# A decoder step on one core: sample keys by sorted lists, low halves of the projection on VectorE

## What is computed

```python
def _select_keys(scores, qpos, kpos, topk):
    admissible = kpos[None, None, :] <= qpos[None, :, None]
    scores = jnp.where(admissible, scores, -jnp.inf)
    _, idx = lax.top_k(scores, topk)
    valid = idx <= qpos[None, :, None]
    return idx, valid
...
    p, new_pool = _pool_mixer(u, pool_buf, pos0, pool_w, pool_scale)
    mix = jnp.concatenate([a, p.astype(a.dtype)], axis=-1)
    x = x + _rmsnorm(jnp.einsum('btm,md->btd', mix, w_o), g_mix_post)
    f, new_conv = _conv_ffn(_rmsnorm(x, g_ffn_pre), conv_buf, w_up, conv_w, conv_b, w_down)
    x = x + _rmsnorm(f, g_ffn_post)
```

## Time and profile before

| What | us |
|---|---|
| median of three runs (lowest, highest) | 1237.61 (1235.37, 1239.82) |
| the profiled execution, its span | 1237.51, 1235.7 |
| TensorE busy | 1165.7 (94%) |
| VectorE busy | 853.7 (69%) |
| ScalarE busy | 540.1 (44%) |
| GpSimd busy, of it low halves | 162.5 (13%), 97.3 |

### The profile page before, as it was taken

One profiled execution on the slowest core, in us unless ns is written; L12 is line 12 of the kernel. 1 busy time (PEld: TensorE's weight loads), 2 busy tenths in 40 slices (PEclk: granted clock), 3 DMA queues, 4 the chain that ended last, 5 costly groups with the idle time before them and its releaser, 6 DMA issues.

```text
span 1235.7 us, 25937 instructions
## 1 busy us (share of the span) xinstructions
PE 1165.7 (94%) x9153; PEld 1121.5 (91%) x9153; DVE 853.7 (69%) x1495; ACT 540.1 (44%) x769; POOL 162.5 (13%) x109
## 2 busy tenths in 40 slices
PE   8999977988989799999999999999999899999993
PEld 7889967966879699999999999999999899999992
DVE  4779899877447877777777777777776444444445
ACT  7333322434224664555545545455454343434341
POOL 4746765200000400000000000000000000000002
PEclk9999988999899999999999999999999899999997
DMA  8987856735885175555555555555556666666641
GB/s 300 319 262 252 274 182 205 252 121 174 293 290 178 36 241 194 168 181 181 166 188 169 179 182 168 187 170 176 185 166 194 203 182 180 179 185 175 185 138 70
DMA packets 81080, 238.76 MB, mean 193 GB/s; under 512 B 9440, under 2 KB 28992, under 8 KB 78704
## 3 DMA queue, kind: packets, MB, share of 16 engines
q1 hardware_dynamic: 75152, 225.40, 57.2%
q10 hardware_dynamic: 4480, 9.01, 2.2%
q0 software_dynamic: 1408, 3.84, 0.9%
HBM read 231.64 MB, written 24.16 MB: 207 GB/s over the span
## 4 chain that ended last, share of the span: by engine, by line
PE 83%; DVE 11%; DMA 3%; ACT 1%; issue 1%; SPq 0%; DVEq 0%; POOL 0%; ACTq 0%; POOLq 0%
PE bank L1312 26%; PE bank L1313 26%; PE bank L1315 26%; DVE lo L406 1%; DMA cache_ring<-vscr 1%; DVE Ws L976 1%; DVE part L1184 1%; DVE top8s L975 1%; DMA raw<-in_w_in 1%; DMA x<-xscr 1%; DVE mixed L1016 1%; PE bank L1488 1%; PE bank L1523 1%; DVE short L1084 1%; DVE mixed L1022 1%
## 5 line engine op out<-in xcount | busy, mean ns | idle before, releaser
L1312 PE MATMUL bank<-h_hi,hi 128*128 128x266 f32 (+1 forms) x2096 | 606.9, 290 | 18.1 <-DVE kT L1040 7.4
L1315 PE MATMUL bank<-h_hi,lo 128*128 128x266 f32 (+1 forms) x2096 | 604.8, 289 | 0.0
L1313 PE MATMUL bank<-h_lo,hi 128*128 128x266 f32 (+1 forms) x2096 | 604.1, 288 | 0.0
L406 DVE TENSOR_TENSOR lo<-raw,hi 128x1024 fp32r<-128x1024 f32 (+2 forms) x322 | 384.1, 1196 | 210.6 <-ACT hi L398 187.2
L398 ACT ACTIVATE hi<-raw 128x1024 fp32r<-128x1024 f32 (+2 forms) x362 | 373.4, 1034 | 320.8 <-PE bank L1315 267.4
L1312 PEld LDWEIGHTS bank<-h_hi,hi 128*128 128x128 f32 x2096 | 399.5, 191 | 23.6 <-issue 19.3
L1313 PEld LDWEIGHTS bank<-h_lo,hi 128*128 128x128 f32 x2096 | 398.1, 190 | 0.1
L1315 PEld LDWEIGHTS bank<-h_hi,lo 128*128 128x128 f32 x2096 | 397.6, 190 | 0.0
L1312 PE MATMUL bank<-g_hi,hi 128*128 128x264 f32 x704 | 200.3, 285 | 5.7 <-DVE lo L406 5.7
L1313 PE MATMUL bank<-g_lo,hi 128*128 128x264 f32 x704 | 201.2, 286 | 0.0
L1315 PE MATMUL bank<-g_hi,lo 128*128 128x264 f32 x704 | 200.3, 284 | 0.0
(11 more groups left out here) (239 smaller groups left out, 788.9 us busy)
## 6 DMA issues: line engine op xcount, KB each, us to landing
raw<-in_w_up SPq DMA_DIRECT2D x176, 512.0 KB, 3.8
raw<-in_w_in SPq DMA_DIRECT2D x56, 512.0 KB, 5.3
raw<-in_w_down SPq DMA_DIRECT2D x64, 448.0 KB, 3.4
raw<-in_w_o SPq DMA_DIRECT2D x32, 512.0 KB, 4.3
raw<-in_w_down SPq DMA_DIRECT2D x32, 512.0 KB, 3.6
kscr<-in_cache_k SPq DMA_DIRECT2D x64, 128.0 KB
vscr<-in_cache_v SPq DMA_DIRECT2D x64, 128.0 KB
mixed<-kscr SPq DMA_DIRECT2D x8, 512.0 KB, 6.5
```

What stands on the lines that cost most here:

```text
L406: ops.tensor_tensor(lo[:, s, 0:width], raw[:, s, 0:width], hi[:, s, 0:width].bitcast(F32), ALU.subtract).then_inc(done, 1)
L1312: mm(out, w_hi, x_hi[:, k, first:], start=(opens and done == 0), stop=False)
L1313: mm(out, w_hi, x_lo[:, k, first:], start=False, stop=False)
L1315: last = mm(out, w_lo, x_hi[:, k, first:], start=False, stop=(closes and done == total))
```

## The change

- **Low halves.** All chunks' low halves are made by VectorE; GpSimd's loop is gone. In front of its work for tile t VectorE makes the two low halves of tile t + 1 (`low_halves`). ScalarE's first high halves of the projection stand a little earlier.
- **Sample keys.** TensorE sums the sample scores into 64 rows of 128 scores: eight lists per sequence. `sample_lists` gives half the lists the opposite sign and puts the scores back in one row per sequence. Sixteen `sort_round`s order all lists at once. `merge_lists` and `merge_quarters` keep maxima and minima of pairs of lists and put them in order by comparisons at halving distance (`compare`); `sample_threshold` finds the 256th score, and three mask steps make the mask, ties by a running sum.
- **Order.** One unit per tile: a prompt round at U0, U1 and U3 to U7 and at the first two query tiles, `sample_lists` at U2, a pooling group at K0 to V1, now in front of the copy, the prompt mask at the third query tile, four sort rounds at each of the next four, `merge_lists` at the last. The first six heads have the rest.

The diff, cut to its core:

```diff
-        if cj < C_PROJ:
-            eng.wait_ge(lo_dve, 4 * r + cj + 1)
-        elif cj < C_WOP:
-            eng.wait_ge(lo_pool, 4 * r + cj - C_PROJ + 1)
-        else:
-            eng.wait_ge(lo_dve, 4 * r + cj - (C_WOP - C_PROJ) + 1)
+        eng.wait_ge(lo_dve, 4 * r + cj + 1)
...
-            with pool.Fori(0, (C_WOP - C_PROJ) // 4) as i:
-                for j in range(4):
-                    lo_chunk(pool, nc.gpsimd, lo_pool, i, C_PROJ + j)
...
+            hi_chunk(ae, 0, C_PROJ)
+            hi_chunk(ae, 0, C_PROJ + 1)
             for h in range(12, 16):
                 relu_head(h, h % 2)
-                hi_chunk(ae, 0, C_PROJ + h - 12)
+                if h < 14:
+                    hi_chunk(ae, 0, C_PROJ + h - 10)
...
-                if t in range(2, 7):
+                if t in range(2, 8):
                     lo_chunk(dve, nc.vector, lo_dve, 0, C_IQ + 2 * t + 2)
                     lo_chunk(dve, nc.vector, lo_dve, 0, C_IQ + 2 * t + 3)
...
+                if h == 13:
+                    lo_chunk(dve, nc.vector, lo_dve, 0, C_PROJ + 2)
+                    lo_chunk(dve, nc.vector, lo_dve, 0, C_PROJ + 3)
...
-            def sample_round(n):
-                src = (Ss if n == 0 else Ws)[:, :]
-                st.link(nc.vector.max(top8s[:, :], src))
-                st.link(nc.vector.match_replace(Ws[:, :], top8s[:, :], src, NEG))
+            def sample_lists():
+                dve.wait_ge(ssum_done, 1)
+                st.then(nc.vector.tensor_copy(Ss[:, PAST:CTX], misc[0:DB, 0:1]))
+                st.link(nc.vector.tensor_scalar(scored, bank[2][:, 0:LIST], con[:, SGN:SGN + 1], None, mul))
+                st.link(nc.vector.stream_shuffle(other, scored, NEXT_ROWS))
+                for c in range(8):
+                    q = slice(32 * (c // 2), 32 * (c // 2) + DB)
+                    src = (other if c % 2 else scored)[q]
+                    st.then(nc.vector.tensor_scalar(Ss[:, LIST * c:LIST * (c + 1)], src, list_sign(c), None, mul))
+                st.wait()
+            def sort_round(n):
+                src = scored if n == 0 else rest
+                st.link(nc.vector.max(ranked[:, 8 * n:8 * n + 8], src))
+                if n < LIST // 8 - 1:
+                    st.link(nc.vector.match_replace(rest, ranked[:, 8 * n:8 * n + 8], src, NEG))
+            def compare(dst, src, d, rows):
+                to, of = (x[0:rows].rearrange("p (n t d) -> p n t d", t=2, d=d) for x in (dst, src))
+                st.then(nc.vector.tensor_tensor(to[:, :, 0, :], of[:, :, 0, :], of[:, :, 1, :], ALU.max))
+                st.link(nc.vector.tensor_tensor(to[:, :, 1, :], of[:, :, 0, :], of[:, :, 1, :], ALU.min))
+            def merge_lists():
+                st.link(nc.vector.tensor_copy(partner[0:64, 0:LIST], ranked[64:128]))
+                for half, pick in ((0, ALU.max), (1, ALU.min)):
+                    st.then(nc.vector.scalar_tensor_tensor(merged[0][0:64, LIST * half:LIST * (half + 1)],
+                                                           partner[0:64, 0:LIST], -1.0, ranked[0:64], mul, pick))
+                st.wait()
+                for n in range(7):
+                    compare(merged[1 - n % 2], merged[n % 2], 64 >> n, 64)
+            def merge_quarters():
+                st.link(nc.vector.tensor_copy(partner[0:32], merged[1][32:64]))
+                st.link(nc.vector.scalar_tensor_tensor(merged[0][0:32], partner[0:32], -1.0, merged[1][0:32],
+                                                       mul, ALU.max))
+                st.link(nc.vector.tensor_scalar(merged[0][0:32], merged[0][0:32], con[0:32, FLIP:FLIP + 1], None, mul))
+            def compare_quarters(n0, n1):
+                for n in range(n0, n1):
+                    compare(merged[1 - n % 2], merged[n % 2], 128 >> n, 32)
+            def sample_threshold():
+                st.link(nc.vector.stream_shuffle(partner[0:32], merged[0][0:32], NEXT_ROWS))
+                st.link(nc.vector.scalar_tensor_tensor(lowest, merged[0][0:DB], -1.0, partner[0:DB], mul, ALU.min))
+                st.link(nc.vector.max(top8s[:, :], lowest))
+                st.link(nc.vector.scalar_tensor_tensor(thr[:, 1:2], Ss[:, PAST:CTX], -1.0, top8s[:, 1:2], mul, ALU.max))
+                st.link(nc.vector.tensor_tensor(thr[:, 1:2], thr[:, 1:2], top8s[:, 0:1], ALU.min))
+                st.link(nc.vector.tensor_scalar(thr[:, 0:1], thr[:, 1:2], -1.0, None, mul))
+            def sample_mask_1():
+                st.link(nc.vector.tensor_scalar(Ws[:, :], Ss[:, :], thr[:, 0:1], None, ALU.is_gt))
+                st.then(nc.vector.reduce_sum(thr[:, 2:3], Ws[:, :], AX.X))
+                st.link(nc.vector.tensor_scalar(among, Ss[:, :], thr[:, 0:1], None, ALU.is_equal))
+            def sample_mask_2():
+                st.link(nc.vector.tensor_tensor_scan(among, among, among, thr[:, 2:3], ALU.add, ALU.max))
+                st.link(nc.vector.tensor_scalar(among, among, float(TOPK_S), None, ALU.is_le))
+            def sample_mask_3():
+                st.link(nc.vector.scalar_tensor_tensor(among, Ss[:, :], thr[:, 0:1], among, ALU.is_equal, mul))
+                st.link(nc.vector.tensor_tensor(Ws[:, :], Ws[:, :], among, ALU.add))
+                nc.vector.tensor_scalar(Ws[:, :], Ws[:, :], -1.0, -MASKED, ALU.add, ALU.mult).then_inc(smask_ready, 1)
...
+            def low_halves(t):
+                for j in range(2):
+                    lo_chunk(dve, nc.vector, lo_dve, 0, C_PROJ + 2 * t + j)
...
             for t in range(U0, U0 + 8):
-                for _ in range(3 if t < 2 else 1 if t < 5 else 0):
+                if t:
+                    low_halves(t + 1)
+                if t == 2:
+                    sample_lists()
+                else:
                     prompt_round(next(rounds_p))
                 ps = tile_ready(t)
...
             for t in range(K0, K0 + 4):
+                low_halves(t + 1)
+                pool_group(t - K0)
                 ps = tile_ready(t)
                 dst = kT[:, t - K0, :] if t < V0 else vT[:, t - V0, :]
-                ins = nc.vector.tensor_tensor(dst, ps[:, 0:T], rms[:, :], mul)
-                ins.then_inc(tile_freed, 1)
-                pool_group(t - K0)
-                if t < V0:
-                    sample_round(next(rounds_s))
+                nc.vector.tensor_tensor(dst, ps[:, 0:T], rms[:, :], mul).then_inc(tile_freed, 1)
             for t in range(Q0, Q0 + HEADS):
                 h = t - Q0
-                sample_round(next(rounds_s))
-                if h:
-                    sample_round(next(rounds_s))
+                if h < HEADS - 1:
+                    low_halves(t + 1)
+                if h < 2:
+                    prompt_round(next(rounds_p))
+                if h == 2:
+                    prompt_mask()
+                if h in range(3, 7):
+                    for n in range(4 * h - 12, 4 * h - 8):
+                        sort_round(n)
+                if h == 7:
+                    merge_lists()
...
                     masked_scores(h + 1)
-                    left = next(rounds_s, None)
-                    if left is not None:
-                        sample_round(left)
-                    if h == HEADS - 2:
-
-                        st.link(nc.vector.tensor_tensor(Ws[:, :], Ss[:, :], Ws[:, :], ALU.not_equal))
-                        nc.vector.tensor_scalar(Ws[:, :], Ws[:, :], -1.0, -MASKED, ALU.add,
-                                                ALU.mult).then_inc(smask_ready, 1)
+                    if h == 0:
+                        merge_quarters()
+                        compare_quarters(0, 4)
+                    if h == 1:
+                        compare_quarters(4, 8)
+                    if h == 2:
+                        sample_threshold()
+                    if h == 3:
+                        sample_mask_1()
+                    if h == 4:
+                        sample_mask_2()
+                    if h == 5:
+                        sample_mask_3()
...
-            mm(bank[2][0:DB, :], iwblk[:, :], relus[:, 0:512], start=True, stop=True)
-            mm(bank[3][0:DB, :], iwblk[:, :], relus[:, 512:1024], start=True, stop=True)
-            mm(misc[0:DB, 0:1], iwblk[:, :], relus[:, 1024:1025], start=True, stop=True).then_inc(ssum_done, 1)
+            for c in range(8):
+                at = Z_AT - list_row(c)
+                mm(bank[2][:, 0:LIST], iwz[:, at:at + P], relus[:, LIST * c:LIST * (c + 1)], start=(c == 0), stop=(c == 7))
+            mm(misc[0:DB, 0:1], iwz[:, Z_AT:Z_AT + DB], relus[:, PAST:CTX], start=True, stop=True).then_inc(ssum_done, 1)
```

More of the change, by code:

```diff
@@ L93, with list_row, list_sign @@
 PAR_W = CBT + 2 * FT
-IDN, ONE, HREP, BLK, EXP8, M8, INV, DIX, EPC, M16, FOUR = 0, 128, 256, 384, 392, 520, 528, 592, 593, 594, 610
-CON_W = 738
+IDN, ONE, HREP, BLK, EXP8, M8, INV, DIX, EPC, M16, SGN, FLIP, FOUR = 0, 128, 256, 384, 392, 520, 528, 592, 593, 594, 610, 611, 612
+CON_W = 740
 GROUPS = 4
+LIST = PAST // 8
+Z_AT = 120
```

(23 more changed lines are left out.)

24 lines of the change are left out of this document (5 added, 19 removed).

## The result

The changed kernel took 1219.95 us (median of four runs, 1217.64 to 1221.1) against 1238.31 for the kernel before, timed with it (1235.37 to 1239.82). The ratio is 0.9852 with a 95% interval from 0.9827 to 0.9877: 1.5% faster. Forecast were 1214.4 and a range from 1207 to 1226. The profiled execution took 1220.88, its span 1219.1, so 1.8 lie around the span as before.

A forecast was written before the change was run, and what follows sets the result against it. In one projection stretch VectorE, late with copies out of PSUM, and not TensorE, was taken as the bound. From 1237.51 us, 22.8 (projection) and 0.3 (heads) were subtracted, giving 1214.4; range 1207 to 1226.

The forecast's parts named there:

- the forecast's own ends: Whole kernel: 1211 to 1219 us, from the heads' ends and 1 to 2 us of lag; chance 0.76.
- rival 1: Query tiles: VectorE becomes the bound, worth 5 to 12 us, giving 1219 to 1226; chance 0.13.
- Part 1, the pace: Projection: TensorE never waits, copies 6.17 then 5.93 us apart, last copy at 212.1; gain 22.8.
- the thinnest place: Q3 to Q6: VectorE's four sort rounds, low halves and copies take 5.85 us against TensorE's 5.93.
- Part 1, the start: Projection's third tile starts at 102.14 as before; moved halves come earlier and nothing is later for it.
- a last copy after 217: Projection's end: a last copy later than this would make the prediction wrong; it was forecast near 212.
- Part 2, the heads: Heads: sorting steps replace VectorE's sample rounds of 2.55 us per head; sum -0.3, ends -2 and +3.
- heads from 8.1 to 9.4 apart: Heads: spacing in us that would show the prediction right; successive heads were 8.75 apart before.
- VectorE as the bound in the query tiles: Same as rival 1: VectorE's lag and tight sort tiles cost 5 to 12 us, 1219 to 1226; chance 0.13.
- The stretching that stays without GpSimd: Pooling groups keep their lengths because GpSimd is not the cause: 1235 to 1239, no change; chance 0.03.
- The weights as the bound: Projection: weight loads set the pace, at 218 GB/s 1239 us, at 210 GB/s 1244, slower; chance 0.04.
- Shorter heads: Heads: all eight shorten by TensorE's 0.9 us wait, 7 us more gained, 1207; chance 0.04.

The follow-up runs named there:

- second profile: Changed kernel unaltered, profiled again on another chip: measured 1218.86 us, profiled execution 1219.08.
- experiment 2: Changed kernel with the first two projection tiles' high and low halves put back among the index heads, as in the kernel before: 1216.89 us.
- experiment 3: Changed kernel with only ScalarE's third and fourth high halves moved back, behind relus 14 and 15: 1218.61 us.
- experiment 5: Changed kernel without the running sum: 1218.71 us; changed kernel with sample steps of heads 0 to 5 moved before the next head's masking: 1216.14.
- the square: Low halves on GpSimd, then VectorE: rounds over 1025 scores 1236.39 to 1238.31, 1250.36 us; sorted lists 1227.21, 1218.86 to 1219.95.
- experiment 4: Changed kernel's sorting with low halves on GpSimd: 1227.21 us; kernel before, rounds kept, with low halves on VectorE: 1250.36.

## Why the prediction was right, and where it was off

Direction and mechanism were right; the time came out 6.5 above the forecast in the first profiled execution (1220.88) and 4.7 in the second (1219.08). The median, 1219.95, lies above the forecast's own ends, 1211 to 1219; it lies in the whole range by the stretch that was added for rival 1, whose mechanism did not come, and that is luck. By the terms of the sum:

| term | forecast | first profile | second profile |
|---|---|---|---|
| third tile starts | 102.14 | 107.17 (+5.0) | 104.62 (+2.5) |
| from there to the last copy | 110.2 | 110.45 (+0.25) | 110.45 (+0.25) |
| heads, first to last reciprocal | 60.4 | 62.48 (+2.1) | 63.34 (+2.9) |
| last reciprocal to the end of the span | 927.7 | 926.84 (-0.9) | 926.63 (-1.1) |

From the last copy to the first reciprocal are 12.15 to 12.16, before and after.

**Part 1, the pace.** Right to 0.25 us in 110. The 0.2 allowed for the score sums' added weight loads, for which the prediction had no row, stands near what came: from the first of these sums to the third tile are 2.01 us, 1.84 before. The copies are 6.17 and 5.93 apart, V0 and V1 run late and Q0 to Q2 catch up as costed. In Q5, the thinnest place, VectorE waited twice for high halves (0.25 and 0.31), copied 6.36 after the tile before, and TensorE still did not wait.

**Part 1, the start: the step that failed.** The prediction let the third tile start at 102.14 "as now", because the moved halves "come earlier than now, under the last index tile; nothing is later for it". They do come earlier, and that is the fault. They wait for weight loads that land when they land, in order, ahead of relus, index sums and index queries for which TensorE waits. Putting them back gave 102.57, within 0.5 of the forecast (experiment 2). Putting back ScalarE's third and fourth high half alone gave nothing (experiment 3), so VectorE's part is enough for the second profile's 2.5. The first profile's further 2.5 went with the late load of the index tile, ScalarE's waits behind it and a longer spell of the half clock; these were not tried one by one. The prediction named a last copy after 217 as a sign against it. The first profile has 217.62, but the sign was drawn for lateness within the projection, and there was none.

**Part 2, the heads.** Forecast -0.3, measured +1.8 and +2.6. The miss is above all head 4, costed at 8.1 (8.74 less 0.6) and measured at 10.66 and 10.47. Two of its terms were wrong. The running sum was taken at 1.21, near an ordinary step of 1025, and took 2.33, close to the other end named, 2.4: 1.1 more. The Trainium skill (DVE: opcode table, instruction layouts, handler registers and perf-mode slots, section Datapath and trigger behaviour) says that the built-in running sum goes at half throughput; by that rule the forecast would have been 1215.5. The trace agrees: 2333 ns against 1217 for the addition of two inputs of the same shape in the same kernel. The other term was put at nothing: the heads were costed from rows at full clock, and TensorE's clock fell to 0.50 in head 4, which by the waits of experiment 5 costs 1.2 to 1.4. The two make up the excess of 2.5 and 2.3. Another such spell lies in head 0 in the first profile (0.50 from 233 to 237 us) and in head 1 in the second, which took 9.62 where 8.4 was costed. Against these stands head 6, which fell by 1.1 where 0.2 was costed. The sign that was named, heads from 8.1 to 9.4 apart, did not come: they are 6.94 to 10.66 apart. The comparisons of strided pairs went at the full rate that was assumed: a pair of steps takes 0.52, where 0.55 was costed.

**The rivals.** VectorE as the bound in the query tiles: its range holds the time, but its mechanism did not come, since TensorE waited for nothing there. The stretching that stays without GpSimd: refuted by both rows of the square, 0.19 without GpSimd's low halves and 2.27 with them. The Trainium skill (SBUF — State Buffer, section SBUF: two separate sides) calls the port pair of the two engines an exclusive lock for a whole instruction; the 2.27 beside the 0.19 agree. The weights as the bound: ScalarE did wait for loads in the projection, but TensorE never did, and the second stretch moved 274 GB/s where the rival took 218 and less. Shorter heads: not in this change; with the steps moved, order alone gave sums from 59.49 to 61.06.

## What to carry to other kernels

When work is moved earlier on an engine that runs in order, ask what it waits for there and what stands behind it, not only whether it has room: in the second profile a low half that waited 3.5 us for its weights in front of an index sum cost TensorE a wait of 3.3, and a spell of half clock came behind it. Before a sort or a smaller method is costed, look where the steps stand: in head 4 moving the steps into a wait of their engine went with 2.6 us less, of which about half is the clock's, and in heads 2 and 3 their place made no difference. And try the parts of a change apart: here one alone gained 9, the other alone cost 13, and together they gained 18.

## What the runs showed of the hardware

A running sum over 1025 values on 8 partitions takes 2.33 us, an addition of as many 1.22. VectorE's two-input step on 128x32 values takes 0.19 with GpSimd silent and 2.27 beside its 128x1024 subtractions, in two kernels; in the second of them the long step ends with GpSimd's instruction (experiment 4). Steps with one input are hit as well: in the kernel before, a mask step on 128x128 begins at 145.38, just behind a pair of GpSimd's low halves at 145.36, and takes 2.46; the next of its line, on twice the columns, begins 0.3 after that pair has ended, and takes 0.29:

```profile
145.38 2.46 DVE L1007 TENSOR_SCALAR W<-W 128x128 f32<-128x128 f32 x1
...
150.43 0.29 DVE L1007 TENSOR_SCALAR W<-W 128x256 f32<-128x256 f32 x1
```

```profile
145.36 4.75 POOL L406 TENSOR_TENSOR lo<-raw,hi 128x1024 fp32r<-128x1024 f32 x2 [1.47 <-ACT hi L398]
```

TensorE's clock was not the same for the same work: in the two profiles of the changed kernel the first heads (10.03 and 8.25 against 9.58 and 9.62) trade about 1 us between them, with the half clock in different places. In head 4 both have it, and the kernel before has it in none of the seven heads measured. A sum of heads from one profile is therefore good to 1 or 1.5 us here: with the same heads it was 62.48 and 63.34, and with the steps moved 59.49, 60.99 and 61.06.
